# Routed rows gated at eviction and added as three bf16 parts

## The reference, cut to what matters

```python
gates = jnp.sum(jax.nn.one_hot(eidx, N_EXPERTS) * wsel[..., None], axis=1)
def expert_step(acc, xs):
    g_w, u_w, d_w, gate = xs
    hid = jax.nn.silu(xt @ g_w) * (xt @ u_w)
    return acc + gate[:, None] * (hid @ d_w), None
acc, _ = lax.scan(expert_step, zeros, (wg, wu, wd, gates.T))
...
x = x + gt2 * (acc + shared)
```

## Time and profile before

| | |
|---|---|
| profiled execution, span from first to last instruction | 1813.6 us |
| timed runs, median of 3 | 1817.68 us (1815.89 to 1819.21) |
| PE busy | 1696.4 us, 94% of the span |
| DVE busy | 861.0 us, 47% |
| ACT busy | 280.8 us, 15% |
| DMA, whole span | 528 MB, mean 291 GB/s |
| DMA in slices 9 to 18 of 40 (MoE of layer 0) | 406 to 421 GB/s |
| chain of waits: PE / DMA / DVE | 84% / 8% / 4% of the span |

### The profile page before, as it was taken

The page is one execution under the profiler, slowest core; times in us unless marked ns, Lnnn a source line. Parts: engine busy times, 40 slices in busy tenths (PEclk is TensorE's granted clock), DMA queues, the critical chain, the costliest instruction groups (busy, mean ns, idle before and its releaser), DMA issues.

```text
span 1813.6 us, 25634 instructions
## 1 busy us (share of the span) xinstructions
PE 1696.4 (94%) x9272; PEld 971.4 (54%) x9272; DVE 861.0 (47%) x2513; ACT 280.8 (15%) x645; POOL 112.4 (6%) x115
## 2 busy tenths in 40 slices
PE   5999998999999999988999888878999999999996
PEld 2664576544444444435776877756544444444443
DVE  3206425455545554435672664335445554555444
ACT  2134313100100010003112112102100010001001
POOL 0000001000000000000000322000100000000000
PEclk9999789999999999998999899779999999999998
DMA  9967853699999999994331000033889999999993
GB/s 390 335 257 298 319 209 134 228 421 419 420 419 417 409 419 420 419 406 168 124 132 70 1 1 1 3 150 121 307 338 419 419 420 411 407 419 419 420 420 135
DMA packets 81235, 528.08 MB, mean 291 GB/s; under 512 B 13104, under 2 KB 13632, under 8 KB 20400
## 3 DMA queue, kind: packets, MB, share of 16 engines
q1 hardware_dynamic: 68256, 496.14, 67.0%
q0 software_dynamic: 9024, 20.03, 3.0%
q10 hardware_dynamic: 3824, 10.20, 1.6%
HBM read 533.04 MB, written 5.86 MB: 297 GB/s over the span
## 4 chain that ended last, share of the span: by engine, by line
PE 84%; DMA 8%; DVE 4%; issue 2%; ACT 1%; POOL 0%; SPq 0%; ACTq 0%; DVEq 0%
PE ps L665 21%; PE ps L463 14%; PE ps L709 12%; PE ps L692 11%; DMA ring<-in_wexp 4%; DMA arena<-in_wexp 3%; PE ps L649 3%; PE ps L426 3%; PE ps L612 2%; DVE arena L1267 2%; PE ps L922 1%; PE ps L435 1%; PE ps L925 1%; PE ps L443 1%; PE ps L532 1%
## 5 line engine op out<-in xcount | busy, mean ns | idle before, releaser
L1273 DVE SCALAR_TENSOR_TENSOR x<-ps,mod,x 128x256 f32<-128x256 f32 (+1 forms) x1024 | 329.1, 363 | 189.3 <-PE ps L709 120.3
L665 PE MATMUL ps<-arena 128*32 128x512 f32 (+2 forms) x1456 | 309.1, 609 | 8.4 <-DMA arena<-in_wexp 8.3
L709 PE MATMUL ps<-arena 128*128 128x288 f32 x960 | 264.8, 417 | 6.4 <-DVE x L1273 4.2
L709 PEld LDWEIGHTS ps<-arena 128*128 128x128 f32 x960 | 172.0, 189 | 139.6 <-issue 94.2
L665 PE MATMUL ps<-ring,arena 128*64 128x512 f32 (+1 forms) x976 | 211.4, 597 | 2.1 <-DMA arena<-in_wexp 2.1
L463 PE MATMUL ps<-h,ring 128*128 128x288 f32 x768 | 196.5, 417 | 2.1 <-ACT h L1022 2.1
L463 PEld LDWEIGHTS ps<-h,ring 128*128 128x128 f32 x768 | 149.0, 195 | 45.5 <-issue 4.2
L665 PEld LDWEIGHTS ps<-arena 128*32 128x32 f32 (+2 forms) x1456 | 92.6, 128 | 150.7 <-issue 150.2
L1267 DVE TENSOR_TENSOR arena<-ps,arena 128x256 f32<-128x256 f32 (+6 forms) x153 | 56.1, 373 | 211.5 <-issue 171.6
L692 PE MATMUL ps<-ring,arena 128*64 128x512 f32 (+2 forms) x624 | 134.4, 620 | 11.2 <-DMA ring<-in_wexp 11.2
L1590 DVE COPY arena<-ps 128x512 f32<-128x512 f32 x60 | 41.5, 692 | 172.2 <-PE ps L692 167.0
(11 more groups left out here) (273 smaller groups left out, 1640.1 us busy)
## 6 DMA issues: line engine op xcount, KB each, us to landing
arena<-in_wexp SPq DMA_DIRECT2D x210, 1024.0 KB, 23.3
ring<-in_wexp SPq DMA_DIRECT2D x180, 1024.0 KB, 23.1
ring<-in_wmod SPq DMA_DIRECT2D x48, 1024.0 KB, 9.6
ring<-in_win SPq DMA_DIRECT2D x26, 1024.0 KB, 4.9
ring<-in_wout SPq DMA_DIRECT2D x8, 1024.0 KB, 4.8
h_rows<-arena ACTq DMA_DIRECT2D x4, 512.0 KB, 2.6
x<-in_x ACTq DMA_DIRECT2D x1, 1152.0 KB, 16.1
out_y<-h SPq DMA_DIRECT2D x2, 576.0 KB, 2.8
```

The costliest lines, as they stand in the source:

```text
L665: last = mm(ps[2][w, :], xgT[:, r % 2, 4 * q + k, w], unit(("gu", l, s0 + i, q))[:, k * 512:(k + 1) * 512], start=(q == 0 and k == 0), sto ...
L709: mm(ps[ADD_BANKS[c]][:, 0:T], yb[:, r % 2, c * 128:(c + 1) * 128], onehot[:, r % 2, :], start=True, stop=True).then_inc(sem["add_ps"], 1)
L1273: return V.scalar_tensor_tensor(out=o, in0=a, scalar=s, in1=b, op0=op0, op1=op1)
```

## The change

`yb` in fp32 becomes three bf16 parts per number, `yparts[:, 0..2]`, in the space of the same three rows of fp32. The gate is multiplied at eviction and not in the one-hot matrix, which becomes bf16 zeros and ones. With y the product in ps[0] or ps[1] and g the row's gate, for each half hf of 512 columns:

- ACT `rows`: top = bf16(g y), with `Identity` and a scale read from `rowg` (semaphore `top_e`);
- DVE `rest`: ps = g y - top, written back into the same PSUM bank (`rest_e`);
- ACT `rows`: mid = bf16(ps) (`mid_e`);
- DVE `lowest`: low = bf16(ps - mid) (`low_e`).

PE `add(r, c)` accumulates three bf16 products (top, mid, low) in the bank, in place of one fp32 product. `down(r)` and `add(r, 0)` wait on `low_e` where they waited on `ya_e` and `yb_e`.

```diff
-    xgb, yb = cv(2, D), rows3[:, 0:2, :]
+    xgb = cv(2, D)
+    yparts = rows3.bitcast(BF16)
...
-    ids_at, onehot = cv(1, T)[:, 0, :], cv(2, T)
+    ids_at, onehot = cv(1, T)[:, 0, :], cv(2, T // 2).bitcast(BF16)
...
                 def down(r):
                     if r:
-                        pe.wait_ge(sem["ya_e"], B + r)
-                        pe.wait_ge(sem["yb_e"], B + r)
+                        pe.wait_ge(sem["low_e"], 2 * (B + r))
...
                 def add(r, c):
-                        pe.wait_ge(sem["ya_e"], B + r + 1)
-                        pe.wait_ge(sem["yb_e"], B + r + 1)
+                        pe.wait_ge(sem["low_e"], 2 * (B + r + 1))
...
-                    mm(ps[ADD_BANKS[c]][:, 0:T], yb[:, r % 2, c * 128:(c + 1) * 128], onehot[:, r % 2, :],
-                       start=True, stop=True).then_inc(sem["add_ps"], 1)
+                    for i in range(3):
+                        at = (r % 2) * D + c * 128
+                        last = mm(ps[ADD_BANKS[c]][:, 0:T], yparts[:, i, at:at + 128], onehot[:, r % 2, :],
+                                  start=(i == 0), stop=(i == 2))
+                    last.then_inc(sem["add_ps"], 1)
...
# ScalarE, rows(r)
-                    A(yb[:, r % 2, 0:512], ps[0][:, :], ACT.Copy).then_inc(sem["ya_e"], 1)
+                    for hf in range(2):
+                        at = (r % 2) * D + hf * 512
+                        A(yparts[:, 0, at:at + 512], ps[hf][:, :], ACT.Identity, scale=rowg[:, r:r + 1])\
+                            .then_inc(sem["top_e"], 1)
+                    for hf in range(2):
+                        at = (r % 2) * D + hf * 512
+                        act.wait_ge(sem["rest_e"], 2 * (B + r) + hf + 1)
+                        A(yparts[:, 1, at:at + 512], ps[hf][:, :], ACT.Copy).then_inc(sem["mid_e"], 1)
...
# VectorE
-                    ts(onehot[:, r % 2, :], ids_at, rowf[:, r:r + 1], rowg[:, r:r + 1], ALU.is_equal, ALU.mult)\
+                    ts(onehot[:, r % 2, :], ids_at, rowf[:, r:r + 1], None, ALU.is_equal)\
...
-                def rows(r):
-                    dve.wait_ge(sem["dn"], B + r + 1)
-                    if r >= 2:
-                        dve.wait_ge(sem["add_ps"], KC * (B + r - 1))
-                    V.tensor_copy(yb[:, r % 2, 512:1024], ps[1][:, :]).then_inc(sem["yb_e"], 1)
+                def rest(r):
+                    for hf in range(2):
+                        at = (r % 2) * D + hf * 512
+                        dve.wait_ge(sem["top_e"], 2 * (B + r) + hf + 1)
+                        stt(ps[hf][:, :], ps[hf][:, :], rowg[:, r:r + 1], yparts[:, 0, at:at + 512],
+                            ALU.mult, ALU.subtract).then_inc(sem["rest_e"], 1)
+
+                def lowest(r):
+                    for hf in range(2):
+                        at = (r % 2) * D + hf * 512
+                        dve.wait_ge(sem["mid_e"], 2 * (B + r) + hf + 1)
+                        tt(yparts[:, 2, at:at + 512], ps[hf][:, :], yparts[:, 1, at:at + 512], ALU.subtract)\
+                            .then_inc(sem["low_e"], 1)
...
                     if r:
-                        rows(r - 1)
+                        rest(r - 1)
                     if r >= 2:
                         for c in range(4, KC):
                             add(r - 2, c)
+                    if r:
+                        lowest(r - 1)
...
                 for c in range(KC):
                     add(NR - 2, c)
-                rows(NR - 1)
+                rest(NR - 1)
+                lowest(NR - 1)
```

More of the change, by code:

```diff
@@ L162 @@
  shu_ps shu_sb shh shd_ps shd_x
- xg0 xg1 trx xta xtb up sg hd trh ht dn ya_e yb_e add_ps add_x
+ xg0 xg1 trx xta xtb up sg hd trh ht dn top_e rest_e mid_e low_e add_ps add_x
  ab_ps ab_act ab_sb ab_e gcum_ps gcum_e gdec
@@ L796, in moe @@
                     s = lambda n: sem[f"over_{n}{l}"]
-                    pe.wait_ge(sem["ya_e"], B + NR)
-                    pe.wait_ge(sem["yb_e"], B + NR)
+                    pe.wait_ge(sem["low_e"], 2 * (B + NR))
                     with pe.Fori(0, NE) as e:
```

## The result

The changed kernel takes 1826.69 us (median of 4 runs, 1823.81 to 1828.29) against 1816.90 us of the kernel before in the same session: ratio 1.0049, 95% interval 1.0037 to 1.0062. It is slower, as forecast, but by 9.8 us and not by 22. The profiled span grew from 1813.6 to 1824.3 us.

The account below looks back on a forecast made before the run. TensorE and the weight DMA were taken to run neck and neck in the rounds. 2 x (5 + 5.4 + 0.5) = 21.8 us on the 1813.6 span gives 1835.4, with 4.1 for the timed median 1839 us; range 1824 to 1864.

Parts of the forecast that it names:

- The products: Adds in each round: twelve bf16 products for four adds take some 1.5 us in place of 2.05, 0.55 less.
- the row-group rule: TensorE: a weight load overlaps running products only where it goes to another row group; four adds would take 2.6 us.
- The chain: A round's end: VectorE's adds stand behind `rest` (0.69 us each), so `take` starts at +3.8, 1.0 us later.
- Up to the dip: Rounds ahead of the dip: slower iterations make the weight stream and the last load 5 us later in each layer.
- the dip: At 600 to 606 us and around 1526 us: traffic falls to 375 and 395 GB/s because slots come late.
- the earlier start that the prediction put at 0.55: Ahead of `down(1)`: the first adds win 0.55 us, taken off the lateness of the weight stream.
- After the last load: End of a layer's rounds: 2.5 us up to `add(28)`, 2.9 more behind `down(29)`; 5.4 us a layer, all paid.
- The clock: A layer's end: two stops of 4 us lower TensorE's clock, 0.5 us a layer; ends -2.6 and +3.
- The cheap `rest`: Rival, 10%: VectorE's `rest` at 0.43 us; iteration and stream unchanged, only the end paid, some 4 a layer: 1826 us.
- Loads that add to the products: Rival, 7%: in TensorE's adds load and product add up, four adds take 2.6 us; 36 a layer, 1890 us.
- a dear `rest`: Rival, 3%: VectorE's `rest` at 1.18 us; iteration grows by 1.45, 9 at the end: 1893 us.
- a clock that falls in every round: Rival, 4%: each 1.5 us stop lowers TensorE's clock, costing some 1.7 us more; 52 a layer, 1921 us.

Follow-up runs that it names:

- with 10 slots: Kernel before and changed kernel, each with 10 slots for weights in place of 13: 1842.06 us (ratio 1.0138) and 1858.15 us (ratio 1.0225).
- with the transposes: 28 unread identity transposes on TensorE ahead of `up(29, 1)`: kernel before 1816.95 us; changed kernel 1825.68; changed kernel with last two rounds in old fp32 form 1813.77.

## Why the prediction was half wrong

- **The products: right.** 1.5 us for twelve was the forecast; the tables start 1.48 us after the first product does. The loads (98 ns) lie beside the products although all go to the same rows. So the trace does not bear out the row-group rule that the prediction weighed (the Trainium skill, TensorE: Matmul & The Clock Gate, Part 3).
- **The chain: right in kind, 0.17 us too long.** `take` came 0.83 later and not 1.0, as VectorE's two `rest` follow each other at 0.67 us and its adds begin at +2.16, not +2.29. The 0.1 and 0.15 us for signals had no row behind them; by the rows above they are about 0.04 and 0.12. With the products an iteration grew by 0.30 and not 0.45.
- **"Up to the dip": the step that failed.** It said that the stream, and with it the last load, comes 5 us later in each layer. The issues did come up to 4.5 to 6 us later (load 120 of the list, counted from the `take` of round 1: issued 4.48 us later, landed 0.12 us later). But just ahead of the dip a load was under way for 14.5 us, three times the 4.9 of a lone one, so several loads stood ahead of it; lateness only shortened that, to 11, and the weights of `up(29, 1)` came 0.3 us earlier. I had read the lower GB/s of the earlier trace rows as slots that come late. GB/s and DMA share do not tell that: 375 GB/s at a share of 0.95 is a place where lateness was hidden, and 362 GB/s at 0.95, with 10 slots, one where it went through. The time from issue to landing does. From 560 to 600 us the traffic falls with it (416, 397, 362 and 338 GB/s before, after, and with 10 slots); what slows the DMA while several loads are still under way is not settled. A gather of rows runs in the dip, but during the gathers of the other rounds of that layer the traffic is 405 to 429 GB/s. This step is 10 of the 12 us missed. The rest is the -0.3 us in front, which may be the earlier start that the prediction put at 0.55, the end (0.9 us over both layers) and scatter.
- **After the last load: right.** 5.4 us a layer, with 0.5 for the clock, was the forecast; 5.7 and 5.2 came. Both stops are there: 4.39 us ahead of `add(28)` (before 0.51) and 3.73 ahead of `add(29)` (before 1.07).
- **The clock: small, as said, but with the wrong lower end.** `up(29, 1)` took 6.58 and 5.34 us after 6.22 and 5.34. The -2.6 us that a warm TensorE was to bring could not be had: with the transposes `down(28)` waited 1.2 to 1.3 us for its load, and the later adds took the rest.
- **The rivals.** The cheap `rest`, at 1826 us, gave the right time for a wrong reason, which is luck: `rest` was not cheap (0.75 us, not 0.43). Its time was right since it, too, left the stream where it was; and by its own terms (5.4 less three times 0.26, and 0.5 for the clock) it should have been 1828. Loads that add to the products, a dear `rest` and a clock that falls in every round are out: 1.5 us for twelve products, 0.75 us, and a granted clock of 1.00 through the rounds.

## What to carry to other kernels

Before you let lateness of an engine reach a stream of loads, compare the time from issue to landing with that of a lone load: the difference is about what the engine may lose before anything lands later, and fewer buffers shorten it. Here some 11 to 15 us against 4.9 hid up to 4 us of lateness, and 6 to 9 against 4.9 did not. Traffic below its peak does not tell whether loads are starved, and a DMA share of 0.95 does not either. Work added behind the last load was paid in full here; work taken away there was won only up to the next load's landing, so look at that time first.

## What was not expected of the hardware

- TensorE's stops of 2.59 to 3.14 us were followed by half clock in 18 of 26 cases a layer, not in all, and those of 1.23 to 1.8 us in none of 26.
- `scalar_tensor_tensor` that reads and writes the same PSUM bank takes 0.07 us more than a `tensor_tensor` from PSUM to SBUF of the same size (754 and 685 ns), and two in a row start 0.67 us apart.
